# Column-block sums of three down-projection weights: from GpSimd additions in on-chip memory to adding transfers in device memory, one stage earlier

## The chip, the cores and the metric

One core of one Trainium2 chip runs the whole program. The metric is the device time of one execution in microseconds (us), as the median of repeated runs. In the texts PE is TensorE, DVE is VectorE, ACT is ScalarE, POOL is GpSimd and SP is SyncE, which in this kernel only issues transfers. "Device memory" is the chip's HBM, "on-chip memory" is SBUF.

## What is computed

The reference is a small language-model forward pass on one sequence of 512 tokens with a model width of 1024, all in float32. A first layer mixes tokens with three mixers (windowed attention, a state-space mixer, a gated delta-rule mixer), then comes a gated feed-forward block; two more layers with other mixers follow, each with a feed-forward block that has a short convolution. What matters here are the three feed-forward blocks. Cut to their core:

```python
# first block
f = (jax.nn.silu(h @ ffn_w_gate[l]) * (h @ ffn_w_up[l])) @ ffn_w_down[l]
x = x + rmsnorm(f, post_ffn_norm[l])
# the two later blocks: a = gated result of an up projection with a short convolution,
# then a @ w_down of the same shape
```

`ffn_w_down` is 2816 x 1024. So there are three down projections a (512 x 2816) times w (2816 x 1024), numbered n = 0, 1, 2 below.

## The kernel before, in words

**Order of stages.** (1) The input projection `w_in` with the three mixers woven into it, about 0 to 255 us of the span; (2) output projection; (3) up(0), the gate and up projection of block 0, followed by down(0), together about 306 to 650 us; (4) the second layer's mixer; (5) up(1) and down(1); (6) the third layer's mixer; (7) up(2) and down(2), which end the program. The engines run five separate instruction streams, each strictly in its own written order, tied by semaphores. In the mixer stages the order in which dense work (letter F) and mixer work (other letters) follow each other is a fixed string, the same on every engine (`first_order`, L258, walked by `walk`, L242).

**Weights.** Each weight arrives in chunks of at most 128 x 2048 float32 (1 MB), by a transfer that SP issues (`load`, L3367) into one of two buffers `raw`. TensorE works on pairs of high and low halves: ACT writes the high half `wH` (L1609), then DVE (L2274) or POOL (L3091) writes the low half `wL` = raw - wH. The set `BY_POOL` (L124) says for which chunks it is POOL: 1, 3 to 18, 52 to 68 and 111 to 116. Every product is then three matmuls (L681 to L683: high by high, high by low, low by high). A dense chunk of the input projection or of an up projection is two column tiles of eight such triples (`feat_side` on the other engines, L1488, which first prepares chunk c and then chunk c + 1). Two buffers each of `raw`, `wH` and `wL` serve in turn, so chunk c + 1 can be cast once TensorE has left chunk c - 1, and the load of chunk c + 2 is issued when the low half of chunk c is written (L3376).

**Down projection.** It is done as a two-by-two block product with seven block products in place of eight (Strassen's scheme in the form of Winograd). The weight is taken as four blocks of 1408 x 512, called b11, b12, b21 and b22; each is eleven blocks of 128 rows, numbered q. The scheme needs four sums of weight blocks (T1 to T4) and four sums of blocks of the activations (S1 to S4). The activation sums are made by POOL in `branch_sums` (L3035) during the up projection and in `down` (L3062) during the down projection. The weight sums are made in the same up projection by three functions:

- `stage` (SP, L3301) loads block row q of the weight, 1 MB, into the on-chip buffer `extra0`; it waits until the sums of q - 1 have been stored.
- `weight_sums` (POOL, L3050 to L3060) does four additions or subtractions of 128 x 512 in place.
- `store` (SP, L3310) writes `extra0` to `w_sums` (L284) in device memory.

Eleven such rounds fill up(n), whose 22 chunks carry them between their loads. The down projection reads `w_sums` back: `load_a` (L3330) for each q loads b11 from the weight and three sums from `w_sums`; `load_b` (L3343) later loads the fourth sum, then b12 and b21. Their buffers are the ring `raw_ring` (L446): raw[1], raw[0], extra1, extra0.

On TensorE `down` (L772) has first four products for each q, then three others. `partial`, `second`, `third`, `fifth` (DVE, L2183 to L2197), `add_f` (DVE, L2675) and `add_x` (POOL, L3069) add the products up after TensorE has written them.

**The first stage on POOL.** `dense` (L3096) runs `feat_side` for chunks 2 to 10, so POOL writes wL of chunk 3 first, then 4, 5 and so on, one for each chunk of TensorE. Between them `short` and `delta` put some mixer work on POOL (L3102, L3145).

Of the kernel before, what the change touches and what calls it, by code (L numbers as in the profile page):

```python
# [277 lines left out]
def build(nc, ins, out):  # L278
# [11 lines left out]
    with ctx:  # L290
# [276 lines left out]
        def sem(name):  # L567
# [7 lines left out]
        low_dve, low_pool = Line(sem("low_half_done_dve")), Line(sem("low_half_done_pool"))  # L575
        turned_pe, turned_hi, turned_lo = Line(sem("turned")), Line(sem("turned_high")), Line(sem("turned_low"))
        D = {n: Line(sem("dma_" + n), 16) for n in (
            "x0", "x1", "x2", "x3", "cols", "pm", "ident", "U", "brow", "lev", "abias", "ssd_nw", "gain", "oneh", "rb", "u_out", "u_rows", "staged", "stored",
            "row", "x_again", "CM", "wuk", "wuv", "far", "near", "cum_out", "cum0", "cum1", "cum2", "cum3", "sgg", "sgw", "sgb", "out")}
        pre, ev, gate, att, ssd, gdn0, gdn1, sums, mix, res, ffn, even, idx, unit, lat, odd, sgu, ln, dn = stages = [  # L580
            Marks(sem, n) for n in ("pre", "evac", "gate", "att", "ssd", "gdn0", "gdn1", "sums", "mix", "res", "ffn", "even", "index",
# [1568 lines left out]
        def dve_program(e):  # L2150
# [25 lines left out]
            def down(n, turn_tile, add_last, centre, finish):  # L2176

                for q in range(1, 11):
                    if q > 2:
                        low_outer(n, q - 3)  # L2180
                    low_a(n, q)

                def partial(name, j, bank, o, a):  # L2183
                    w.wait_ge(*dn.pe.at(n, bank[0], j))
                    e.tensor_tensor(o, a, q4v(ps[bank[1] + j][:, :]), ALU.add).then_inc(*dn.dve.one(n, name, j))

                def second(j):
                    w.wait_ge(*dn.act.at(n, "P1", j))
                    partial("P6", j, ("P6", 6), part(j, 1), part(j, 0))

                def third(j):
                    w.wait_ge(*dn.dve.at(n, "P6", j))
                    partial("P7", j, ("P7", 0), part(2 + j, 0), part(j, 1))

                def fifth(j):
                    w.wait_ge(*dn.dve.at(n, "P7", j))
                    partial("C22", j, ("P5", 2), part(2 + j, 1), part(2 + j, 0))  # L2197

                low_outer(n, 8)
                low_b(n, 0)  # L2200
                low_b(n, 1)
                second(0)
                second(1)
                low_outer(n, 9)
                third(0)
                third(1)
                low_b(n, 2)
                fifth(0)
                low_b(n, 3)
                fifth(1)  # L2210
                low_outer(n, 10)
                for v in range(4, 8):
                    low_b(n, v)
                add_last(2, 0, "P4", 6)
                low_b(n, 8)
                centre(2)
                finish(2)
                low_b(n, 9)
                add_last(3, 0, "P4", 6)
                low_b(n, 10)  # L2220
                centre(3)
                finish(3)
                for v in range(11, 14):
                    low_b(n, v)
                turn_tile(2)
                low_b(n, 14)
                low_b(n, 15)
                turn_tile(3)
                low_b(n, 16)
                add_last(0, 0, "P2", 4)  # L2230
                add_last(0, 1, "P3", 2)
                if n == 0:
                    split_done.add(51)
                    finish(0)
                    low_half(51, 0)
                    low_half(51, 1)
                    add_last(1, 0, "P2", 4)
                    add_last(1, 1, "P3", 2)
                elif n == 1:
                    split_done.update((101, 102))  # L2240
                    low_half(101, 0)
                    centre(0)
                    low_half(101, 1)
                    finish(0)
                    add_last(1, 0, "P2", 4)
                    low_half(102, 0)
                    add_last(1, 1, "P3", 2)
                    low_half(102, 1)
                    centre(1)
                else:  # L2250
                    centre(0)
                    finish(0)
                    add_last(1, 0, "P2", 4)
                    add_last(1, 1, "P3", 2)
                    centre(1)
                finish(1)
# [418 lines left out]
            def add_f(i, h, name, bank):  # L2675
                w.wait_ge(*dn.pe.at(0, name, i % 2))
                if i > 1 or h:
                    w.wait_ge(*dn.dve.at(0, "C22", i % 2))
                    e.tensor_tensor(part(i, h), part(i, h), q4v(ps[bank + i % 2][:, :]), ALU.add).then_inc(*dn.dve.one(0, name, i % 2))
                if i > 1:  # L2680
                    scale_f(i, 1)
                scale_f(i, h)
                if i > 1 or h:
                    w.wait_ge(*res.act.at("f", "sq", i, 0 if i > 1 else 1))
                    e.tensor_tensor(st[:, 24 + i:25 + i], st[:, 16 + 2 * i:17 + 2 * i], st[:, 17 + 2 * i:18 + 2 * i], ALU.add).then_inc(*res.dve.one("f", "sum", i))
# [345 lines left out]
        def pool_program(e):  # L3031
            w = Waits(e)
            split_done = set()

            def branch_sums(n, c0):  # L3035

                for m in range(22):
                    k = m % 11
                    if m % 2 == 0 and m < 20 or m == 19:
                        weight_sums(n, (m + 1) // 2)  # L3040
                    w.wait_ge(*ffn.dve.at("a", c0 + m))
                    if m < 11:
                        e.tensor_tensor(aR[:, k, 512:768], aR[:, k, 256:512], aR[:, k, 512:768], ALU.subtract).then_inc(*dn.pool.one(n, "S3", k))  # L3043
                    else:
                        w.wait_ge(*dn.pool.at(n, "S3", k))
                        e.tensor_tensor(aR[:, k, 768:1024], aR[:, k, 1280:1536], aR[:, k, 512:768], ALU.subtract).then_inc(*dn.pool.one(n, "S2", k))  # L3046
                        w.wait_ge(*dn.pool.at(n, "S2", k))
                        e.tensor_tensor(aR[:, k, 0:256], aR[:, k, 768:1024], aR[:, k, 256:512], ALU.add).then_inc(*dn.pool.one(n, "S1", k))

            def weight_sums(n, q):  # L3050

                b11, b12, b22, b21 = (extra0[:, 512 * j:512 * j + 512] for j in range(4))
                w.wait_ge(*D["staged"].at(n, q))
                e.tensor_tensor(b22, b22, b12, ALU.subtract).then_inc(*dn.pool.one(n, "T3", q))  # L3054
                w.wait_ge(*dn.pool.at(n, "T3", q))
                e.tensor_tensor(b12, b12, b11, ALU.subtract).then_inc(*dn.pool.one(n, "T1", q))
                w.wait_ge(*dn.pool.at(n, "T1", q))
                e.tensor_tensor(b11, b22, b11, ALU.add).then_inc(*dn.pool.one(n, "T2", q))
                w.wait_ge(*dn.pool.at(n, "T2", q))
                e.tensor_tensor(b21, b21, b11, ALU.subtract).then_inc(*dn.pool.one(n, "T4", q))  # L3060

            def down(n):  # L3062

# [5 lines left out]
                def add_x(i):  # L3069
                    if n:  # L3070
                        w.wait_ge(*ffn.act.at("x", n - 1, i))
                        w.wait_ge(*(dn.dve.at(n, "C22", i - 2) if i > 1 else dn.dve.at(n, "wlo", 12 + i)))
                        for h in (1, 0) if i > 1 else (1,):
                            xv = x[:, i, 512 * h:512 * h + 512]
                            e.tensor_tensor(q4v(xv), q4v(xv), part(i, h), ALU.add).then_inc(*dn.pool.one(n, "x", i, h))

                for i in HI_FIRST:
                    add_x(i)
# [16 lines left out]

            def dense():  # L3096
                for j in range(9):
                    yield from feat_side(C_IN + j, split, none)
                yield from tok_side([C_Z, C_Z + 1], True, split, none)
                yield "done"  # L3100
# [192 lines left out]
        def sp_program(e):  # L3293
# [4 lines left out]
                o = offs[DOWN[n]] + q * 128 * 2048  # L3298
                return ins["wbig"][o:o + 128 * 2048].rearrange("(p n) -> p n", p=128)[:, c0:c1]

            def stage(n, q):  # L3301

                if q:
                    w.wait_ge(*D["stored"].at(n, q - 1))
                else:
                    for p in [*(conv_start(n - 1) if n else ffn_start()), chunk_done(DOWN[n] - 23)]:
                        w.wait_ge(*p)
                e.dma_start(extra0[:, :], blocks(n, q, 0, 2048)).then_inc(*D["staged"].one(n, q))

            def store(n, q):  # L3310
                w.wait_ge(*dn.pool.at(n, "T4", q))
                e.dma_start(w_sums[n, q], extra0[:, :]).then_inc(*D["stored"].one(n, q))

            def up(n, c0, extra=None):

                split(c0)
                stage(n, 0)
                lead_side(c0, split, none, none)
                if extra:
                    extra(1)  # L3320
                for m in range(2, 22):
                    if m % 2 == 0 and m < 20 or m == 19:
                        store(n, (m + 1) // 2 - 1)
                        stage(n, (m + 1) // 2)
                    run(feat_side(c0 + m, split, none))
                    if extra:
                        extra(m)
                store(n, 10)

            def load_a(n, q):  # L3330

# [3 lines left out]
                    w.wait_ge(*ffn.dve.at("a", DOWN[n] - 1))  # L3335
                elif q > 3:
                    w.wait_ge(*dn.dve.at(n, "w23", q - 4))
                w.wait_ge(*D["stored"].at(n, 10 if q == 3 else q))
                line = raw_landed[A_RAW[q]]
                e.dma_start(raw_a(q)[:, 0:512], blocks(n, q, 0, 512)).then_inc(*line.one("first", n, q))  # L3340
                e.dma_start(raw_a(q)[:, 512:2048], w_sums[n, q, :, 0:1536]).then_inc(*line.one("a", n, q))
# [1 line left out]
            def load_b(n, r):  # L3343
# [1 line left out]
                w.wait_ge(*(dn.dve.at(n, "w23", 7 + r) if r < 4 else dn.dve.at(n, "wlo", (1, 3, 5, 7, 9)[r - 4])))  # L3345
                line = raw_landed[B_RAW[r]]
                if r < 3:
                    w.wait_ge(*D["stored"].at(n, 10))
                    ks, o, src = range(4 * r, min(4 * r + 4, 11)), 512, w_sums[n, :, :, 1536:2048].rearrange("k p n -> p k n")
                else:  # L3350
                    ks, o = range(2 * r - 6, min(2 * r - 4, 11)), 1024
# [308 lines left out]
```

## Time and profile before

| | |
|---|---|
| median of 3 runs | 1785.3 us (1784.28 to 1785.46) |
| the profiled execution's own time | 1785.67 us |
| span of the profiled execution, first to last instruction | 1783.8 us |
| outside the span | 1.9 us |
| busy, share of the span | PE 98%, DVE 65%, ACT 44%, POOL 37% |
| transfers | 270.83 MB, 152 GB/s over the span |
| mean granted clock of TensorE | 0.997 of full |

The span is what the rows below cover; all stages are placed by microseconds from its start. The 1.9 us outside are before the first and after the last instruction.

### The profile page before, as it was taken

The page shows a single profiled execution, that of the slowest core. Times are in us where ns is not written, and L with a number is a line of the kernel's source. Part 1 is how long each engine was busy: PE and PEld are TensorE (multiplying, and loading weights), DVE is VectorE, ACT ScalarE, POOL GpSimd, SP SyncE. Part 2 cuts the span into 40 slices and gives each one's busy share as a digit, 9 for nine tenths or more (in the row PEclk, how much of TensorE's full clock was granted, in tenths as well). Part 3 has the DMA queues.
Part 4 walks back from the last instruction along what each step waited for, and adds up shares of the span by engine and source line. Part 5 has one row for each costly group of instructions (what it writes and reads, how often), then busy time and mean ns, then how long its engine had stood idle before and what let it go on. Part 6 is the DMA issues. An engine that isn't in the chain of part 4 may idle for free.

```text
span 1783.8 us, 23185 instructions
## 1 busy us (share of the span) xinstructions
PE 1754.1 (98%) x9476; PEld 1448.8 (81%) x9476; DVE 1157.7 (65%) x1564; ACT 784.0 (44%) x1203; POOL 660.9 (37%) x434
## 2 busy tenths in 40 slices
PE   8999989999999999999999999999999999999998
PEld 7788978888888888666788888888788898888886
DVE  4687655323347857867657666689674467667798
ACT  6665345222225644556434433465333234333562
POOL 1443533332553114431243445532101344455431
PEclk9999999999999999999999999999999999999999
DMA  5212032654656533330225555574332245555663
GB/s 190 82 60 73 8 120 87 220 199 160 244 212 216 191 113 136 109 122 24 72 95 189 192 195 192 200 263 172 118 115 104 85 166 189 195 198 196 260 202 109
DMA packets 56548, 270.83 MB, mean 152 GB/s; under 512 B 5577, under 2 KB 11761, under 8 KB 34170
## 3 DMA queue, kind: packets, MB, share of 16 engines
q1 hardware_dynamic: 52090, 264.11, 41.8%
q10 hardware_dynamic: 4352, 5.24, 0.8%
q8 instruction: 75, 1.23, 0.3%
q14 instruction: 31, 0.25, 0.0%
HBM read 232.60 MB, written 38.30 MB: 152 GB/s over the span
## 4 chain that ended last, share of the span: by engine, by line
PE 91%; DVE 5%; ACT 2%; DMA 1%; issue 1%; POOL 1%; SPq 0%; ACTq 0%; DVEq 0%
PE ps L681 26%; PE ps L683 26%; PE ps L682 26%; PE ps L678 1%; PE ps L677 1%; PE ps L676 1%; PE ps L1312 1%; PE ps L1278 1%; PE ps L765 1%; PE ps L1271 1%; PE ps L1265 1%; DMA extra<-w_sums 1%; POOL wL L3091 1%; ACT wH L1609 1%; PE ps L1237 1%
## 5 line engine op out<-in xcount | busy, mean ns | idle before, releaser
L681 PE MATMUL ps<-hH,wH 128*128 128x512 f32 (+1 forms) x1560 | 593.5, 380 | 2.2 <-DVE gT L2321 0.9
L683 PE MATMUL ps<-hH,wL 128*128 128x512 f32 (+1 forms) x1560 | 587.0, 376 | 0.0
L682 PE MATMUL ps<-hL,wH 128*128 128x512 f32 (+1 forms) x1560 | 586.8, 376 | 0.0
L3091 POOL TENSOR_TENSOR wL<-raw,wH 128x1024 fp32r<-128x1024 f32 (+2 forms) x80 | 188.8, 2382 | 424.9 <-ACT wH L1609 417.4
L681 PEld LDWEIGHTS ps<-hH,wH 128*128 128x128 f32 x1560 | 293.9, 188 | 59.2 <-issue 3.4
L683 PEld LDWEIGHTS ps<-hH,wL 128*128 128x128 f32 x1560 | 293.6, 188 | 54.1
L682 PEld LDWEIGHTS ps<-hL,wH 128*128 128x128 f32 x1560 | 293.8, 188 | 51.6 <-issue 0.2
L1609 ACT ACTIVATE wH<-raw 128x1024 fp32r<-128x1024 f32 (+2 forms) x226 | 223.0, 1036 | 151.6 <-PE ps L683 143.9
L2274 DVE TENSOR_TENSOR wL<-raw,wH 128x1024 fp32r<-128x1024 f32 (+1 forms) x146 | 232.8, 1633 | 41.4 <-ACT wH L1609 41.4
L2884 DVE SCALAR_TENSOR_TENSOR ft<-ps,cols,ft 128x511 f32<-128x511 f32 (+1 forms) x176 | 131.6, 748 | 149.0 <-ACT ft L2063 145.8
L2063 ACT ACTIVATE ft<-ps,cols 128x512 f32<-128x512 f32 x88 | 60.6, 689 | 189.3 <-PE ps L683 189.3
L681 PE MATMUL ps<-wH,hH 128*128 128x512 f32 (+2 forms) x320 | 113.2, 354 | 3.3 <-DVE x L2917 1.6
L3054 POOL TENSOR_TENSOR extra<-extra 128x512 f32<-128x512 f32 x33 | 43.4, 1315 | 186.2 <-DMA extra<-in_wbig 186.2
L683 PE MATMUL ps<-wH,hL 128*128 128x512 f32 (+2 forms) x320 | 110.5, 345 | 0.0
L682 PE MATMUL ps<-wL,hH 128*128 128x512 f32 (+2 forms) x320 | 110.4, 345 | 0.0
L681 PE MATMUL ps<-wH,agH 128*128 128x512 f32 x264 | 102.9, 390 | 0.5 <-DVE wL L2160 0.5
L682 PE MATMUL ps<-wL,agH 128*128 128x512 f32 x264 | 102.7, 389 | 0.0
L683 PE MATMUL ps<-wH,agL 128*128 128x512 f32 x264 | 102.7, 389 | 0.0
L2663 DVE TENSOR_TENSOR aR<-ft,ps 128x512 f32<-128x512 f32 x22 | 15.1, 688 | 133.9 <-PE ps L683 133.9
L3067 POOL TENSOR_TENSOR aR<-aR 128x256 f32<-128x256 f32 x33 | 50.1, 1524 | 94.1 <-DVE agL L2165 94.1
L3043 POOL TENSOR_TENSOR aR<-aR 128x256 f32<-128x256 f32 x33 | 44.3, 1343 | 99.4 <-DVE aR L2893 68.8
L3046 POOL TENSOR_TENSOR aR<-aR 128x256 f32<-128x256 f32 x33 | 45.2, 1368 | 92.5 <-DVE aR L2893 59.1
(430 smaller groups left out, 2850.3 us busy)
## 6 DMA issues: line engine op xcount, KB each, us to landing
raw<-in_wbig SPq DMA_DIRECT2D x114, 1024.0 KB, 5.6
extra<-in_wbig SPq DMA_DIRECT2D x42, 1024.0 KB, 4.8
w_sums<-extra SPq DMA_DIRECT2D x33, 1024.0 KB, 8.7
raw<-w_sums SPq DMA_DIRECT2D x21, 768.0 KB, 6.5
extra<-w_sums SPq DMA_DIRECT2D x15, 768.0 KB, 7.1
rows<-in_rows SPq DMA_DIRECT2D x11, 512.0 KB, 8.0
raw<-in_wbig SPq DMA_DIRECT2D x18, 256.0 KB, 5.6
x<-in_x SPq DMA_DIRECT2D x8, 512.0 KB, 5.0
```

The source lines that it names most:

```text
L681: e.matmul(o, hi, m_hi, start=first, stop=False)
L682: e.matmul(o, hi, m_lo, start=False, stop=False)
L683: return e.matmul(o, lo, m_hi, start=False, stop=end)
L1609: e.activation(wH[r][:, cs], raw[r][:, cs], ACT.Copy).then_inc(*cast.one(c, h))
L2063: e.activation(ft[s][:, :], ps[b0 + t][:, :], ACT.Identity, scale=cols[:, column + 2:column + 3]).then_inc(*ffn.act.one("y", c, t))
L2274: e.tensor_tensor(wL[r][:, cs], raw[r][:, cs], wH[r][:, cs].bitcast(F32), ALU.subtract).then_inc(*low_dve.one(c, h))
L2884: e.scalar_tensor_tensor(y[:, d:512], ps[b0 + t][:, 0:512 - d], cols[:, column + 2 - d:column + 3 - d], y[:, d:512], ALU.mult, ALU.add).th ...
L3043: e.tensor_tensor(aR[:, k, 512:768], aR[:, k, 256:512], aR[:, k, 512:768], ALU.subtract).then_inc(*dn.pool.one(n, "S3", k))
L3046: e.tensor_tensor(aR[:, k, 768:1024], aR[:, k, 1280:1536], aR[:, k, 512:768], ALU.subtract).then_inc(*dn.pool.one(n, "S2", k))
L3054: e.tensor_tensor(b22, b22, b12, ALU.subtract).then_inc(*dn.pool.one(n, "T3", q))
L3067: e.tensor_tensor(aR[:, k, 768:1024], aR[:, k, 1024:1280], aR[:, k, 768:1024], ALU.subtract).then_inc(*dn.pool.one(n, "S4", k))
L3091: e.tensor_tensor(wL[r][:, cs], raw[r][:, cs], wH[r][:, cs].bitcast(F32), ALU.subtract).then_inc(*low_pool.one(c, h))
```

## The change

The sums are now made in device memory, by transfers that POOL issues. A plain transfer copies within device memory; a transfer with `accum_op=ALU.add` adds its source to what stands at its destination. Since these only add, the scheme is written so that all weight sums have plus signs: T1 = b11 + b12, T3 = b22 + b12, T2 = T3 + b11, T4 = T2 + b21 (before: differences). The signs go over to the activation sums and to the additions behind the products; the number, shape and engine of those instructions stay.

For each n there are twelve transfers, k = 0 to 11: six steps, each in two halves (block rows 0 to 5 and 6 to 10; 768 and 640 rows of device memory). Steps 0, 2 and 4 copy, steps 1, 3 and 5 add; steps 0 and 1 move two pieces of 512 numbers for each row, the others one. Each half has its own semaphore, and POOL waits for a half's previous step before it issues the next. For n = 0 they stand in `dense` of the first stage, two ahead of each of the chunks j = 1 to 6. For n = 1 and 2 they stand in `branch_sums` of up(0) and up(1), one ahead of each of the first twelve activation sums. `stage`, `store` and `weight_sums` are gone from SP and POOL.

```diff
-            "x0", ..., "u_rows", "staged", "stored",
+            "x0", ..., "u_rows", "block_sums0", "block_sums1",
...
-                def partial(name, j, bank, o, a):
+                def partial(name, j, bank, o, a, op=ALU.add):
...
-                    partial("P6", j, ("P6", 6), part(j, 1), part(j, 0))
+                    partial("P6", j, ("P6", 6), part(j, 1), part(j, 0), ALU.subtract)
...
-                    partial("C22", j, ("P5", 2), part(2 + j, 1), part(2 + j, 0))
+                    w.wait_ge(*dn.pe.at(n, "P5", j))
+                    e.tensor_tensor(part(2 + j, 1), q4v(ps[2 + j][:, :]), part(2 + j, 0), ALU.subtract).then_inc(*dn.dve.one(n, "C22", j))
...
-                    e.tensor_tensor(part(i, h), part(i, h), q4v(ps[bank + i % 2][:, :]), ALU.add).then_inc(*dn.dve.one(0, name, i % 2))
+                    if name == "P3":
+                        e.tensor_tensor(part(i, h), q4v(ps[bank + i % 2][:, :]), part(i, h), ALU.subtract).then_inc(*dn.dve.one(0, name, i % 2))
+                    else:
+                        e.tensor_tensor(part(i, h), part(i, h), q4v(ps[bank + i % 2][:, :]), ALU.add).then_inc(*dn.dve.one(0, name, i % 2))
...
+            def block_sums(n, k):
+
+                step, half = k // 2, k % 2
+                qs = slice(6 * half, 6 + 5 * half)
+                line = D[f"block_sums{half}"]
+                w_rows = ins["wbig"][offs[DOWN[n]]:offs[DOWN[n] + 1]].rearrange("(q p n) -> q p n", q=11, p=128)[qs].rearrange("q p n -> (q p) n")
+                s_rows = w_sums[n, qs].rearrange("q p n -> (q p) n")
+                t2, t1, t3, t4 = (slice(512 * a, 512 * a + 512) for a in range(4))
+                b11, b12, b22, b21 = t2, t1, t3, t4
+                if step:
+                    w.wait_ge(*line.at(n, step - 1))
+                if step == 0:
+                    o, a = s_rows[:, 512:1536].rearrange("r (h n) -> r h n", h=2), w_rows[:, 0:2048].rearrange("r (h n) -> r h n", h=2)[:, :, 0:512]
+                elif step == 1:
+                    o, a = s_rows[:, 512:1536].rearrange("r (h n) -> r h n", h=2), w_rows[:, b12].unsqueeze(1).broadcast_to([s_rows.shape[0], 2, 512])
+                else:
+                    o, a = ((s_rows[:, t2], s_rows[:, t3]), (s_rows[:, t2], w_rows[:, b11]),
+                            (s_rows[:, t4], s_rows[:, t2]), (s_rows[:, t4], w_rows[:, b21]))[step - 2]
+                if step in (1, 3, 5):
+                    e.dma_start(o, a, accum_op=ALU.add).then_inc(*line.one(n, step))
+                else:
+                    e.dma_start(o, a).then_inc(*line.one(n, step))
...
                 for m in range(22):
                     k = m % 11
-                    if m % 2 == 0 and m < 20 or m == 19:
-                        weight_sums(n, (m + 1) // 2)
+                    if n < 2 and m < 12:
+                        block_sums(n + 1, m)
...
-                        e.tensor_tensor(aR[:, k, 768:1024], aR[:, k, 1280:1536], aR[:, k, 512:768], ALU.subtract).then_inc(*dn.pool.one(n, "S2", k))
+                        e.tensor_tensor(aR[:, k, 768:1024], aR[:, k, 1280:1536], aR[:, k, 512:768], ALU.add).then_inc(*dn.pool.one(n, "S2", k))
                         w.wait_ge(*dn.pool.at(n, "S2", k))
-                        e.tensor_tensor(aR[:, k, 0:256], aR[:, k, 768:1024], aR[:, k, 256:512], ALU.add).then_inc(*dn.pool.one(n, "S1", k))
-
-            def weight_sums(n, q):
...
+                        e.tensor_tensor(aR[:, k, 0:256], aR[:, k, 256:512], aR[:, k, 768:1024], ALU.subtract).then_inc(*dn.pool.one(n, "S1", k))
...
-                            e.tensor_tensor(q4v(xv), q4v(xv), part(i, h), ALU.add).then_inc(*dn.pool.one(n, "x", i, h))
+                            e.tensor_tensor(q4v(xv), q4v(xv), part(i, h), ALU.add if i > 1 else ALU.subtract).then_inc(*dn.pool.one(n, "x", i, h))
...
             def dense():
                 for j in range(9):
+                    if 1 <= j < 7:
+                        block_sums(0, 2 * j - 2)
+                        block_sums(0, 2 * j - 1)
                     yield from feat_side(C_IN + j, split, none)
...
-            def stage(n, q):
...
-            def store(n, q):
...
-                stage(n, 0)
...
-                    if m % 2 == 0 and m < 20 or m == 19:
-                        store(n, (m + 1) // 2 - 1)
-                        stage(n, (m + 1) // 2)
...
-                store(n, 10)
...
                 elif q > 3:
                     w.wait_ge(*dn.dve.at(n, "w23", q - 4))
-                w.wait_ge(*D["stored"].at(n, 10 if q == 3 else q))
+                elif q == 3:
+                    for p in conv_start(n - 1) if n else ffn_start():
+                        w.wait_ge(*p)
+                w.wait_ge(*D[f"block_sums{q // 6}"].at(n, 3))
...
-                    w.wait_ge(*D["stored"].at(n, 10))
+                    for half in range(2):
+                        w.wait_ge(*D[f"block_sums{half}"].at(n, 5))
```

## Rows read from the trace of the kernel before

**Rows 1.** Busy time, share of the span and instructions of each engine.
```profile
PE 1754.1 (98%) x9476; PEld 1448.8 (81%) x9476; DVE 1157.7 (65%) x1564; ACT 784.0 (44%) x1203; POOL 660.9 (37%) x434
```
**Rows 2.** Windows: stretch; its length, busy per engine (instructions); clock; DMA share, GB/s.
```profile
240.00:250.00 10.00, 6.05 (x42) 5.21 (x42) 8.61 (x20) 3.72 (x10) 0.00 (x0) 0.82 0.03 11
250.00:255.00 5.00, 4.47 (x18) 3.52 (x17) 2.78 (x5) 3.59 (x5) 1.28 (x1) 0.68 0.34 115
...
306.00:546.00 240.00, 238.79 (x1128) 200.78 (x1127) 85.13 (x71) 62.02 (x73) 100.05 (x79) 1.00 0.54 196
545.00:650.00 105.00, 105.00 (x473) 86.99 (x471) 87.13 (x87) 65.08 (x83) 19.21 (x13) 1.00 0.54 193
...
920.00:1160.00 240.00, 239.59 (x1136) 201.66 (x1135) 159.76 (x157) 92.76 (x119) 117.29 (x77) 1.00 0.54 191
```
**Rows 3.** Waits of PE over the span, by releaser: total us, times, longest.
```profile
PE ps L862 <- DMA rows<-in_rows: 5.1, 1, 5.1
...
PE ps L681 <- POOL wL L3091: 0.8, 2, 0.4
```
**Rows 4.** Groups of POOL instructions by line: xcount, busy us, mean ns, idle before.
```profile
L3060 POOL TENSOR_TENSOR extra<-extra 128x512 f32<-128x512 f32 x33 | 56.5, 1713 | 2.6
...
L3054 POOL TENSOR_TENSOR extra<-extra 128x512 f32<-128x512 f32 x33 | 43.4, 1315 | 186.2 <-DMA extra<-in_wbig 186.2
```
**Rows 5.** POOL's timeline in the first stage: start us, length us, instructions.
```profile
36.84 4.76 POOL L3091 TENSOR_TENSOR wL<-raw,wH 128x1024 fp32r<-128x1024 f32 x2 [16.13 <-ACT wH L1609]
49.17 4.77 POOL L3091 TENSOR_TENSOR wL<-raw,wH 128x1024 fp32r<-128x1024 f32 x2 [7.57 <-ACT wH L1609]
63.05 5.22 POOL L3091 TENSOR_TENSOR wL<-raw,wH 128x1024 fp32r<-128x1024 f32 x2 [9.11 <-ACT wH L1609]
...
73.29 4.74 POOL L3091 TENSOR_TENSOR wL<-raw,wH 128x1024 fp32r<-128x1024 f32 x2
88.52 4.75 POOL L3091 TENSOR_TENSOR wL<-raw,wH 128x1024 fp32r<-128x1024 f32 x2 [10.49 <-ACT wH L1609]
105.20 5.19 POOL L3091 TENSOR_TENSOR wL<-raw,wH 128x1024 fp32r<-128x1024 f32 x2 [11.93 <-ACT wH L1609]
...
122.49 4.77 POOL L3091 TENSOR_TENSOR wL<-raw,wH 128x1024 fp32r<-128x1024 f32 x2
```
**Rows 6.** PE's timeline, the first matmul of each of chunks 4 to 9.
```profile
59.62 0.48 PE L681 MATMUL ps<-hH,wH 128*128 128x512 f32 x1
...
70.60 0.39 PE L681 MATMUL ps<-hH,wH 128*128 128x512 f32 x1
...
86.62 0.47 PE L681 MATMUL ps<-hH,wH 128*128 128x512 f32 x1
...
103.10 0.48 PE L681 MATMUL ps<-hH,wH 128*128 128x512 f32 x1
...
116.68 0.39 PE L681 MATMUL ps<-hH,wH 128*128 128x512 f32 x1
...
133.40 0.39 PE L681 MATMUL ps<-hH,wH 128*128 128x512 f32 x1
```
**Rows 7.** Transfers over the span: xcount, KB each, median us from issue to landing.
```profile
raw<-in_wbig SPq DMA_DIRECT2D x114, 1024.0 KB, 5.6
...
w_sums<-extra SPq DMA_DIRECT2D x33, 1024.0 KB, 8.7
```
**Rows 8.** Transfers, 428.9 to 440 us: busy tenths, GB/s in 40 slices; one issue.
```profile
DMA  0099409999997711111159799999921111111111
GB/s 0 0 236 177 118 0 413 472 443 443 384 413 325 295 59 44 55 44 55 50 227 428 310 458 463 458 458 458 428 79 44 44 44 44 44 44 50 44 44 44
...
u_rows<-u_scratch SPq DMA_DIRECT2D x1, 384.0 KB
```
**Rows 9.** Up(0): an issue of SP, a cast of ACT.
```profile
428.63 0.33 SPq L3377 DMA_DIRECT2D raw<-in_wbig  x1
...
435.01 2.01 ACT L1609 ACTIVATE wH<-raw 128x1024 fp32r<-128x1024 f32 x2 [4.90 <-PE ps L683]
```

More of the change, by code:

```diff
@@ L577, in build @@
         D = {n: Line(sem("dma_" + n), 16) for n in (
-            "x0", "x1", "x2", "x3", "cols", "pm", "ident", "U", "brow", "lev", "abias", "ssd_nw", "gain", "oneh", "rb", "u_out", "u_rows", "staged", "stored",
+            "x0", "x1", "x2", "x3", "cols", "pm", "ident", "U", "brow", "lev", "abias", "ssd_nw", "gain", "oneh", "rb", "u_out", "u_rows", "block_sums0", "block_sums1",
             "row", "x_again", "CM", "wuk", "wuv", "far", "near", "cum_out", "cum0", "cum1", "cum2", "cum3", "sgg", "sgw", "sgb", "out")}
@@ L2181, in down @@
                     low_a(n, q)
-                def partial(name, j, bank, o, a):
+                def partial(name, j, bank, o, a, op=ALU.add):
                     w.wait_ge(*dn.pe.at(n, bank[0], j))
-                    e.tensor_tensor(o, a, q4v(ps[bank[1] + j][:, :]), ALU.add).then_inc(*dn.dve.one(n, name, j))
+                    e.tensor_tensor(o, a, q4v(ps[bank[1] + j][:, :]), op).then_inc(*dn.dve.one(n, name, j))
                 def second(j):
                     w.wait_ge(*dn.act.at(n, "P1", j))
-                    partial("P6", j, ("P6", 6), part(j, 1), part(j, 0))
+                    partial("P6", j, ("P6", 6), part(j, 1), part(j, 0), ALU.subtract)
                 def third(j):
@@ L3045, in branch_sums @@
                         w.wait_ge(*dn.pool.at(n, "S3", k))
-                        e.tensor_tensor(aR[:, k, 768:1024], aR[:, k, 1280:1536], aR[:, k, 512:768], ALU.subtract).then_inc(*dn.pool.one(n, "S2", k))
+                        e.tensor_tensor(aR[:, k, 768:1024], aR[:, k, 1280:1536], aR[:, k, 512:768], ALU.add).then_inc(*dn.pool.one(n, "S2", k))
                         w.wait_ge(*dn.pool.at(n, "S2", k))
-                        e.tensor_tensor(aR[:, k, 0:256], aR[:, k, 768:1024], aR[:, k, 256:512], ALU.add).then_inc(*dn.pool.one(n, "S1", k))
-            def weight_sums(n, q):
[L3052 to L3060, printed above, removed]
+                        e.tensor_tensor(aR[:, k, 0:256], aR[:, k, 256:512], aR[:, k, 768:1024], ALU.subtract).then_inc(*dn.pool.one(n, "S1", k))
             def down(n):
@@ L3299, in blocks @@
                 return ins["wbig"][o:o + 128 * 2048].rearrange("(p n) -> p n", p=128)[:, c0:c1]
-            def stage(n, q):
[L3303 to L3308, printed above, removed]
-            def store(n, q):
-                w.wait_ge(*dn.pool.at(n, "T4", q))
-                e.dma_start(w_sums[n, q], extra0[:, :]).then_inc(*D["stored"].one(n, q))
             def up(n, c0, extra=None):
                 split(c0)
-                stage(n, 0)
                 lead_side(c0, split, none, none)
```

## The prediction

> **What bounds the kernel now.** I read the busy shares first: PE is busy 1754.1 of 1783.8 us [rows 1], so every change that only frees another engine has 29.7 us to win over the whole program. The windows say where that is not: in up(0) and down(0) PE idles 1.2 us of 345, in up(1) 0.4 of 240 [rows 2]. These are the stages from which POOL's additions and SP's staging transfers go. The waits of PE name POOL with 0.8 us in all; the longest single one, 5.1 us, is for a first load at the start, which the change does not touch [rows 3]. So the bound is TensorE's own stream, and the question is whether the new work, which is waited for on POOL, reaches it.
>
> **What goes.** 4 x 33 POOL instructions of 1.3 to 1.7 us [rows 4], about 196 us of POOL time, all in up stages. They released only the stores. 33 loads and 33 stores on SP go with them. Value on the path: at most the 1.6 us of idle in these windows [rows 2]; I take 0. The first load of the down projection's ring that could have waited for the last store waits anyway for the last activation tile or stands behind one that does. The changed signs keep number, engine and shape of every addition: 0. The added wait for P5 in `fifth` was inside `partial` before: 0.
>
> **What comes, by size.** A float is 4 bytes. Steps 0 and 1 write 768 x 2 x 512 numbers = 3.15 MB in the first half and 2.62 MB in the second; steps 2 to 5 write 1.57 and 1.31 MB. For one n that is 23 MB written, half of it by copies, half by adding.
>
> *Rate of a copy.* The only copy within device memory, u_rows, kept two of the sixteen engines busy (a tenth) at 44 to 47 GB/s, so 22 to 23.5 each; sixteen would give up to 376 GB/s, if nothing behind them is shared. That is the upper end. The same rows show at most 463 GB/s in one direction when all sixteen work [rows 8]. A copy reads and writes, an addition reads twice and writes. If those streams share some 460 GB/s, and the weight loads keep taking 1.05 MB for each chunk of some 14 us (75 GB/s), then about 380 is left: 190 GB/s of copied and 127 GB/s of added bytes. The lower end is a store's median, 1.05 MB in 8.7 us or 120 GB/s, landing time and queueing included [rows 7]; for adding, half of that, 60. I take 190 and 127, as they come from a rate seen with all sixteen engines; both ends stay for the range. A landing adds 2 to 3 us to the moving (a 1.05 MB load lands in 5.6 us [rows 7], at 420 to 460 GB/s it moves in 2.4); I take 2.
>
> The Trainium skill (DMA: Bandwidth & Descriptors, the table of latency and other measured facts) gives 214 GB/s per direction as the full rate of copies between tensors in device memory. By it my sum below would be about 13 us smaller than with 190; no row here shows such a copy on sixteen engines.
>
> *Price of an issue on POOL.* No row has one. SP's take 0.33 us [rows 9]; that is the low end. POOL must also make a read and a write entry for each of up to 1536 pieces of 2 KB. Its fastest of the four old sums pays 1315 ns for 512 columns [rows 4], 2.6 ns each; I take 1 us + 2.5 ns a piece: 4.8 and 4.2 us for steps 0 and 1, 2.9 and 2.6 us for the rest. High end: 7.5 ns a piece.
>
> **First stage, n = 0: the place that decides.** Behind each waiting transfer POOL's queue holds wL of the next chunk, for which PE waits. POOL writes wL(4) at 49.2, wL(5) at 63.1, wL(6) at 73.3, wL(7) at 88.5, wL(8) at 105.2, wL(9) at 122.5 [rows 5]; PE starts those chunks at 59.6, 70.6, 86.6, 103.1, 116.7, 133.4 [rows 6]. It needs only the first of the two instructions, 2.6 us. Slack: 59.6 - 51.8 = 7.8 us, then 4.9, 10.7, 12.0, 8.9, 8.3. The mixer's other instructions on POOL (5 us before wL(6), some 8 before wL(9)) shift along.
>
> Transfers run one after the other on the engines; a pair of one step can be passed only when both halves of the step before have landed.
> - Step 0: issued 41.6 (end of wL(3)) to 50.6; moved by 59.2 and 73.0; landed 61 and 75. wL(4) at 50.6: no stall.
> - Step 1: issued 61 and 75; POOL is free at 79.2. wL(5)'s first half is there at 81.8, needed at 70.6: **stall 11.2**. Moving takes 24.8 + 20.7 us: landed 99.7 and 120.4.
> - Step 2: second half issued at 120.4; wL(6) at 125.6, needed at 86.6 + 11.2 = 97.8: **stall 27.8** (39.0 so far). Moved by 133.5, landed 135.5.
> - Step 3: issued by 138.1; wL(7) at 140.7, needed at 142.1: none. Landed 147.9 and 158.2.
> - Step 4: issued by 160.8; wL(8) at 163.4, needed at 155.7: **stall 7.8**. Landed 173.4.
> - Step 5: issued by 179.2, behind the mixer's instructions; wL(9) at 181.8, needed at 180.1: **stall 1.6**.
>
> Sum 48.4 us. A long idle also costs clock: at 240 to 255 us, after PE had fallen under two thirds busy, the granted clock was 0.82 for 10 us and 0.68 for 5 [rows 2], a loss of 0.18 x 10 + 0.32 x 5 = 3.4 us between the two levels (1.2 and 2.4 GHz). Three stalls: up to 10. Against it, other chains catch up meanwhile and part of the 4.5 us that PE idles at 240 to 255 [rows 2] may shrink; I take 4 off. **Sum: 48.4 + 10 - 4 = 54 us slower.** Against the profiled execution's own 1785.67 (span 1783.8 and 1.9 around it) that is 1840; the median, 1785.3, is 0.4 lower, so 1840 stands.
>
> **Up stages, n = 1 and 2.** The same waits stand on POOL, before activation sums that nobody needs until the down projection. Ten transfers must land before POOL is through: 11.5 MB copied at 190 and 8.7 added at 127 are 61 + 68 us, with landings about 150, well inside the 240 us of the stage. Cost 0. Weight loads share the engines: one issued at 428.6 is cast on ACT at 445.9, two casts after 424.1 with 10.9 us between them [rows 9], so 17.3 us for a landing of 5.6; cover of nearly 12. If that cover went, each load too late by 1 us would cost PE that microsecond, over about twelve chunks twice.
>
> **Rivals.**
> (a) *Hidden anyway; not slower.* Place: POOL between wL(3) and wL(5). If copies keep u_rows' rate on sixteen engines (376 GB/s) and adding runs at 250 or more, step 0 lands by 53 and 59 us, step 1 by 75, and the stalls are 0 to 2 us: 1785 to 1787. It decides at the pass of step 1: stalls start when its second issue ends later than about 68 us. For it: the first stage moves only some 75 GB/s. Against it: the share argument. Between this and the forecast, 376 with 188 gives 9 us and 300 with 200 gives 11: 1790 to 1800.
> (b) *Adding far slower.* 120 with 80 or 60 GB/s gives stalls of 121 or 157 us, with clock 1915 to 1955; the up stages then last 205 to 240 us on POOL, just inside. With 190 and half of it, 95, the stalls sum to 71 us: 1865. The Trainium skill (Collectives: The Full Stack, on why a reducing step runs at half the gathering one) lays such a half rate to two reads on one ring; by it the last figure holds.
> (c) *POOL's own issue time.* With 7.5 ns a piece and fast transfers (376 both) stalls are 44 us, at 10 ns 72: the same end by another road, 1835 to 1870. It would show as long busy issues in place of waits.
> (d) *PE fills the gaps with mixer work.* The written order excludes it: behind the first matmul of a chunk everything on PE waits too. No chance given.
>
> **How the numbers follow.** A measurement of this kernel tells about 0.2% (3.6 us) from no change. Faster by more needs idle time that the removed work caused; the windows leave 2 us: 0.03. Rival (a) proper: 0.17. Slower by more: 0.80, made of 0.17 between (a) and the forecast, 0.40 for the forecast and (c) (1810 to 1875), 0.23 above that, a third of which I leave out past 1935. Range 1785 to 1935; the likeliest case alone 1810 to 1875.
>
> **What would show it.** Right: POOL waits for transfers before L3091 between 55 and 180 us, PE's waits name POOL wL L3091 with tens of us, chunk 6 starts near 125, and both up stages keep 240 us. Wrong: step 1 landed by 80 us; or long POOL issues; or PE idle in up(0), which would mean that weight loads starve. The pattern of the copies' GB/s in the first stage settles the rates.

## The result, and the profile after

The changed kernel takes 1838.95 us (median of 4 runs, 1835.57 to 1841.73) against 1785.38 us: a ratio of 1.0298, 95% interval 1.0286 to 1.0310. The forecast was 1840. The profiled execution has a span of 1833.7 us, 49.9 more than before. It is the shortest of the four, so the rows below explain 49.9 of the 53.6 us between the medians.

The total is as forecast, but it is not made up as forecast. Half of it arose where I had put nothing. The views show that in this order.

The busy shares of the kernel after (they answer to [rows 1]):
```profile
PE 1762.0 (96%) x9476; PEld 1453.0 (79%) x9476; DVE 1120.9 (61%) x1564; ACT 783.4 (43%) x1203; POOL 514.9 (28%) x338
```
POOL's busy time fell by 146 us: some 196 us of additions went, and the issues of the 36 transfers, which are counted here, brought about 50. PE's idle time grew from 29.7 to 1833.7 - 1762.0 = 71.7 us, by 42.0; its busy time grew by 7.9 us with the same number of instructions, as its granted clock was lower (0.984 over the span against 0.997 before, 0.77 from 60 to 110 us, where the longest wait lies). 42.0 + 7.9 = 49.9.

Windows of the kernel after: the first stage and the output projection up to up(0), up(0) itself, and the rest (columns as in [rows 2]):
```profile
0.00:320.00 320.00, 284.05 (x2211) 241.85 (x2212) 184.25 (x330) 154.62 (x285) 127.51 (x87) 0.95 0.54 153
...
355.00:595.00 240.00, 219.48 (x951) 180.81 (x950) 68.92 (x60) 52.52 (x61) 40.96 (x41) 0.96 0.64 170
595.00:1834.00 1239.00, 1225.14 (x6071) 999.05 (x6069) 849.38 (x1153) 558.67 (x831) 328.20 (x203) 1.00 0.43 140
```
In up(0) PE idles 20.5 us; [rows 2] had 1.2. From 595 us on it idles 13.9 us, as before (1238.0 - 1224.59 = 13.4 for the same stretch). A landmark gives the shares of the 49.9 us. POOL writes wL of the same chunk, at the end of the output projection, at 295.65 before and here:
```profile
320.40 5.37 POOL L3106 TENSOR_TENSOR wL<-raw,wH 128x1024 fp32r<-128x1024 f32 x2 [14.21 <-ACT wH L1609]
```
So 24.8 us are lost by then, 21.1 of them idle time of PE and 3.6 longer matmuls. The first cast of down(0) on ACT stands at 583.4 here and 533.8 before, so up(0) adds another 24.8 us (20.5 and 4.3); the first cast of down(1) is 49.5 late, and nothing is added there. Up(1), with the same twelve transfers, costs nothing.

Waits of PE over the span after (as [rows 3]):
```profile
PE ps L681 <- DVE wL L2275: 22.2, 3, 12.5
PE ps L681 <- POOL wL L3106: 19.1, 4, 16.5
PE ps L862 <- DMA rows<-in_rows: 5.1, 1, 5.1
```
Two causes of nearly the same size: low halves from POOL (forecast) and low halves from DVE (not forecast).

**First stage.** POOL's timeline after (as [rows 5]; the lines with DMA_DIRECT2D are the issues, L3060 a copy, L3058 an addition; the time in brackets is how long POOL sat idle before, and for what):
```profile
39.88 3.33 POOL L3060 DMA_DIRECT2D w_sums<-in_wbig  x2
49.04 4.76 POOL L3106 TENSOR_TENSOR wL<-raw,wH 128x1024 fp32r<-128x1024 f32 x2 [5.83 <-ACT wH L1609]
56.68 3.17 POOL L3058 DMA_DIRECT2D w_sums<-in_wbig  x1 [2.88 <-DMA w_sums<-in_wbig]
67.23 2.71 POOL L3058 DMA_DIRECT2D w_sums<-in_wbig  x1 [7.38 <-DMA w_sums<-in_wbig]
68.74 5.90 POOL L3106 TENSOR_TENSOR wL<-raw,wH 128x1024 fp32r<-128x1024 f32 x2
...
88.29 0.76 POOL L3060 DMA_DIRECT2D w_sums<-w_sums  x1 [8.61 <-DMA w_sums<-in_wbig]
104.38 0.68 POOL L3060 DMA_DIRECT2D w_sums<-w_sums  x1 [15.33 <-DMA w_sums<-in_wbig]
105.07 4.66 POOL L3106 TENSOR_TENSOR wL<-raw,wH 128x1024 fp32r<-128x1024 f32 x2
```
The reader is to see the second issue of each pair waiting for a transfer, and wL, in the queue behind it, following at once: wL(5) at 68.7 (before 63.1), wL(6) at 105.1 (before 73.3). PE's timeline has the price:
```profile
107.56 0.77 PE L681 MATMUL ps<-hH,wH 128*128 128x512 f32 x1 [16.46 <-POOL wL L3106]
```

**Up(0).** ACT's casts wait for weight loads:
```profile
432.56 2.00 ACT L1609 ACTIVATE wH<-raw 128x1024 fp32r<-128x1024 f32 x2 [21.21 <-DMA raw<-in_wbig]
...
479.73 2.00 ACT L1609 ACTIVATE wH<-raw 128x1024 fp32r<-128x1024 f32 x2 [25.76 <-DMA raw<-in_wbig]
```
The two loads were issued at 398.0 and 440.6. The first one's line in its source view (the landing is from issue to data):
```profile
L3381 SPq DMA_DIRECT2D raw<-in_wbig x1: 9534/9534/9534, 398.0 to 398.0; - x1
...
DMA to landing us min/median/max: 34.6/34.6/34.6
```
The issue of this load alone kept SP busy for 9.5 us (9534 ns); most others take 0.33. The second load took 39.1 us. The two loads that follow these two took 27.7 and 31.7. All others of up(0) from 354 us until the sums are done land in 8.5 to 11.1 us, and those of up(1), beside the same steps, in 8.2 to 10.8. The price on PE, which needs the low half that DVE makes from such a load:
```profile
435.02 0.76 PE L681 MATMUL ps<-hH,wH 128*128 128x512 f32 x1 [7.98 <-DVE wL L2275]
...
482.19 0.77 PE L681 MATMUL ps<-hH,wH 128*128 128x512 f32 x1 [12.54 <-DVE wL L2275]
```
What SP had issued just ahead of the slow two, 10.5 and 4.2 us earlier, is in its timeline:
```profile
387.47 0.73 SPq L3458 DMA_DIRECT2D u_rows<-u_scratch  x1
...
436.41 0.62 SPq L3458 DMA_DIRECT2D u_rows<-u_scratch  x1
```
These are the first two of four copies on two of the sixteen transfer engines [rows 8]; the other two come when the sums are nearly or quite done, and up(1) has none. That gave theory A: the first stage is late by POOL's queue, up(0) by u_rows meeting POOL's transfers.

### The profile page after: what moved, and what is told of

Read it like the earlier page. It is cut to its first block, busy times and chain, and to the rows that moved or that the text cites. A ratio compares the mean times of both kernels' runs of the same rounds, so it can differ in the third digit from the quotient of the medians.

```text
span 1833.7 us, 23033 instructions
## 1 busy us (share of the span) xinstructions
PE 1762.0 (96%) x9476; PEld 1453.0 (79%) x9476; DVE 1120.9 (61%) x1564; ACT 783.4 (43%) x1203; POOL 514.9 (28%) x338
## 4 chain that ended last, share of the span: by engine, by line
PE 83%; DMA 8%; DVE 5%; ACT 2%; POOL 1%; issue 1%; SPq 0%; ACTq 0%; DVEq 0%
PE ps L681 24%; PE ps L683 23%; PE ps L682 23%; DMA raw<-in_wbig 4%; DMA w_sums<-in_wbig 3%; PE ps L678 1%; PE ps L676 1%; PE ps L677 1%; PE ps L1312 1%; PE ps L1278 1%; POOL wL L3106 1%; ACT wH L1609 1%; PE ps L765 1%; PE ps L1271 1%; PE ps L1265 1%
## 5 line engine op out<-in xcount | busy, mean ns | idle before, releaser
L681 PE MATMUL ps<-hH,wH 128*128 128x512 f32 (+1 forms) x1560 | 596.6, 382 | 42.5 <-DVE wL L2275 20.5
L2275 DVE TENSOR_TENSOR wL<-raw,wH 128x1024 fp32r<-128x1024 f32 (+1 forms) x146 | 198.6, 1400 | 79.6 <-ACT wH L1609 79.6
L3073 POOL TENSOR_TENSOR aR<-aR 128x256 f32<-128x256 f32 x33 | 44.4, 1345 | 277.9 <-DVE aR L2897 168.4
L3070 POOL TENSOR_TENSOR aR<-aR 128x256 f32<-128x256 f32 x33 | 39.2, 1189 | 164.5 <-DVE aR L2897 134.9
L3082 POOL TENSOR_TENSOR aR<-aR 128x256 f32<-128x256 f32 x33 | 51.0, 1552 | 93.5 <-DVE agL L2165 93.5
L681 PEld LDWEIGHTS ps<-wH,hH 128*128 128x128 f32 x320 | 60.8, 190 | 12.1 <-DVE wL L2275 1.9
```

Of the source, the lines that this page charges most:

```text
L681: e.matmul(o, hi, m_hi, start=first, stop=False)
L2275: e.tensor_tensor(wL[r][:, cs], raw[r][:, cs], wH[r][:, cs].bitcast(F32), ALU.subtract).then_inc(*low_dve.one(c, h))
L3082: e.tensor_tensor(aR[:, k, 768:1024], aR[:, k, 1024:1280], aR[:, k, 768:1024], ALU.subtract).then_inc(*dn.pool.one(n, "S4", k))
```

## The experiments

All times are medians; ratios are to the kernel before on the same chip. Eight kernels ran.

### Apart: u_rows on sixteen engines, sums in their own stage

The first edit turns the order of the dimensions of the four u_rows copies:

```diff
-   e.dma_start(bass.AP(u_rows.tensor, h * 128 * 385, [[128 * 385, 2], [385, 128], [1, 384]]),
-               bass.AP(u_dram.tensor, h * 384, [[384, 2], [0, 128], [1, 384]]))
+   e.dma_start(bass.AP(u_rows.tensor, h * 128 * 385, [[385, 128], [128 * 385, 2], [1, 384]]),
+               bass.AP(u_dram.tensor, h * 384, [[0, 128], [384, 2], [1, 384]]))
```


> The changed kernel, but the four u_rows copies of up(0) have their dimension of 128 rows outermost, so that all sixteen transfer engines share them; same bytes. Theory A: the second half of the loss (24.8 us by landmarks, in up(0)) comes from weight loads queued behind u_rows on the two engines that u_rows uses, where it must share with POOL's adding transfers. Then up(0) keeps 240 us, weight loads there land within 12 us, and the median is 1838.95 - 24.8 = about 1814 us; the first stage stays 24.8 us late. Rival B: POOL's transfers starve the weight loads by bandwidth, with or without u_rows: landings of 30 us stay and the time stays at 1830 or more.

Measured: 1812.96 us, ratio 1.0157 (1.0143 to 1.0171), 26.0 us less than the changed kernel. The first stage of its profiled execution is 27.0 us late by the landmark above. Weight loads in up(0) land in 8.4 to 11.7 us while the sums run, and in up(0) PE waits for DVE's wL no more. The forecast of theory A held; so the traffic of the sums by itself is covered, and rival B falls.

The second edit makes each n's twelve transfers in its own stage, up(n), and so takes those of n = 0 out of the first stage:
```diff
-                    if n < 2 and m < 12:
-                        block_sums(n + 1, m)
+                    if m < 12:
+                        block_sums(n, m)
...
-                    if 1 <= j < 7:
-                        block_sums(0, 2 * j - 2)
-                        block_sums(0, 2 * j - 1)
```


> The changed kernel with each n's twelve transfers in its own up stage (n in up(n)), none in the first stage. Theory A: the first stage returns to its times of before (wL of chunk 6 at 73 us), up(0) keeps its loss of some 25 us as u_rows still uses two engines: 1810 to 1816 us; the sums land some 150 us into the stage, 90 before they are read. Rival B': the first stage's delay is from something else that came with the change (PE chunk 6 still starts 20 us or more late, 1835). Rival C: sums made in their own stage come too late for the down projection, and its first product waits by 5 us or more.

Measured: 1796.16 us, 1.0065 (1.0050 to 1.0079). The first stage is back where it was (the landmark stands at 295.69). My figure was missed: 10.9 us are lost between the medians, not 25. The profiled execution, the shortest of the four, is 7.8 us longer than before, and PE waits for wL from DVE for 5.8 of them in up(0). The load behind the first u_rows (at 362.7 us) landed in 19.1 us, the one behind the second (397.8) in 32.4, the one behind the third (442.2) in 18.7. So 24.8 is not a constant of the stage. What sets the size stays open. The steps that stand beside u_rows do not tell it alone: the first u_rows comes 2.8 us before POOL passes step 1's first half and 22.8 before it passes the second, in the changed kernel 2.5 and 20.4, and yet the load behind it took 19.1 us here and 34.6 there. The sums come in time: no wait of PE for one releaser from down(0) on sums to more than 1.8 us, and rival C falls too.

Both edits together:

> Both edits of the two runs before: sums in their own up stage, u_rows on sixteen engines. Theory A: the two losses are the whole loss and add: 1785 to 1787 us, within 0.2% of the kernel before, with POOL busy some 145 us less than in the kernel before. If a third loss exists it is what remains above 1787. A gain of more than 2 us would mean that the staging of before had cost something that its waits did not show; I expect none.

Measured: 1785.21 us, 1.0002 (0.9993 to 1.0011), from 11 runs. PE waits for the same things in this run as in the kernel before; POOL is named with 0.8 us, as before. The three largest:
```profile
PE ps L862 <- DMA rows<-in_rows: 5.0, 1, 5.0
PE ps L1007 <- DVE yall L2450: 3.3, 2, 2.8
PE ps L1271 <- DVE least L2799: 1.8, 4, 1.0
```
and its busy shares are
```profile
PE 1754.1 (98%) x9476; PEld 1448.6 (81%) x9476; DVE 1110.7 (62%) x1564; ACT 783.6 (44%) x1203; POOL 511.5 (29%) x338
```
PE's 1754.1 is the number of before to the digit. So the two losses are the whole loss, and making the sums by transfers frees 149 us of POOL with no measurable change of the time.

> The kernel before with u_rows alone put on sixteen engines. Theory A: there u_rows costs nothing, as no adding transfers share its two engines and the cover of 12 us suffices: within 1 us of the kernel before, 1785. If u_rows already cost something, it is faster by that.

Measured: 1785.37 us, 0.9999 (0.9990 to 1.0009). In the kernel before, u_rows on two engines cost nothing that can be measured.

### What the first stage pays for

Both runs here stand on the first one (u_rows on sixteen engines, 1812.96 us). In this one the adding steps copy, so the sums are not made, while source, destination and bytes written stay:
```diff
-                    e.dma_start(o, a, accum_op=ALU.add).then_inc(*line.one(n, step))
+                    e.dma_start(o, a).then_inc(*line.one(n, step))
```


> e1 (changed kernel with u_rows on sixteen engines, 1812.96 us) with the three adding steps made plain copies of the same source and destination; so the weight sums are left out and the kernel computes something else in the down projections. Theory: in the first stage POOL's wait is as long as the transfers take, and an addition takes longer than a copy as it reads twice: the traces so far give about 235 GB/s of copied and 155 of added bytes, and the forecast's chain worked with 235 for both gives 10 us of stalls in place of 24: about 1799 us, and landings of steps 1 and 3 shorter by a third. Rival: the waits are set by something other than the bytes read (issue, order): 1810 or more.

Measured: 1795.52 us, 1.0057 (1.0041 to 1.0074). The same landmark as above stands at 305.81, 10.2 us late in place of 27.0 in the run that it stands on; my chain with both rates at 235 had 10 of stalls. PE's longest wait for POOL's wL is 5.6 us in place of 19.1, and wL(6) comes at 91.4:
```profile
90.75 0.67 POOL L3060 DMA_DIRECT2D w_sums<-w_sums  x1 [9.31 <-DMA w_sums<-in_wbig]
91.44 4.66 POOL L3106 TENSOR_TENSOR wL<-raw,wH 128x1024 fp32r<-128x1024 f32 x2
```
Step 1, issued at 57.4 and 67.3, landed at 80.4 and 90.4; as an addition, in the changed kernel, it landed at 88.0 and 104.1. POOL's issue of step 1 fell as well, from 3.17 to 1.67 us; the edit changes both at once, but 1.5 us is small beside the 14 us of landing. So the length of the additions carries more than half of the first stage's delay.

Here the low halves of chunks 4 to 9 go to DVE:
```diff
-BY_POOL = {1} | set(range(3, 19)) | ...
+BY_POOL = {1, 3} | set(range(10, 19)) | ...
```


> e1 with the low halves of chunks 4 to 9 written by DVE in place of POOL; the transfers and their waits stay where they are. Theory: the first stage is late because wL stands behind the waits in POOL's queue. Then with wL elsewhere its delay goes, less what 12 more DVE instructions of 1.2 us cost there: 1786 to 1795 us. Rival: the transfers slow the weight loads or the engines themselves: 1805 or more.

Measured: 1799.76 us, 1.0083 (1.0068 to 1.0099): between the theory's range and the rival's. No wait for wL from POOL is left in the first stage, which is 17.3 us late here in place of 27.0 (12.2 of more idle time of PE, 5.1 of longer matmuls). In its place stands the next thing behind POOL's waits:
```profile
PE ps L1065 <- POOL XT L3185: 8.9, 1, 8.9
```
and POOL's timeline of this run shows why:
```profile
130.01 0.72 POOL L3060 DMA_DIRECT2D w_sums<-w_sums  x1 [9.54 <-DMA w_sums<-in_wbig]
139.32 0.68 POOL L3060 DMA_DIRECT2D w_sums<-w_sums  x1 [8.59 <-DMA w_sums<-in_wbig]
139.98 0.54 POOL L3180 MEMSET P<- 128x512 f32 x1
...
141.19 1.27 POOL L3185 TENSOR_TENSOR XT<-lev,XT 128x512 f32<-128x512 f32 x1
```
The mixer's XT, at 111.8 us in the kernel before, comes at 141.2. So POOL's queue still holds PE up, by something else than wL, and no wait of PE names a weight load. The rest of the idle time is in waits for DVE, the largest 1.9 and 2.4 us (0.9 of the latter before); why they grew was not looked into. I had expected the wL to be all that PE waits for there.

### What up(0) pays for

> The changed kernel with u_rows still on two engines, but issued after chunks 16 to 19 of up(0), when POOL's twelve transfers have landed. Theory A: the cost in up(0) is the meeting of the two; apart they cost nothing: 1813 us as e1. Rival: two busy engines alone delay weight loads past their cover: 1825 or more.

The edit is `if m in (16, 17, 18, 19)` in place of `(5, 8, 11, 14)`, with h as 2 * (m - 16). Measured: 1812.47 us, 1.0154 (1.0139 to 1.0169). Loads land in 11.2 us or less. Without the sums beside it a copy on two engines costs nothing that can be measured; the loss needs both.

In the last one the same four copies, with the pattern of before (two parts) and three of them while the sums run, are issued by ACT in its loop over m in place of SP:
```diff
             for m in range(2, 22):
                 run(feat_side(C_UP + m, split, ffn_tile(C_UP + m, 2 * (m % 2))))
+                if m in (5, 8, 11, 14):
+                    h = 2 * (m - 5) // 3
+                    e.dma_start(bass.AP(u_rows.tensor, h * 128 * 385, [[128 * 385, 2], [385, 128], [1, 384]]),
+                                bass.AP(u_dram.tensor, h * 384, [[384, 2], [0, 128], [1, 384]])).then_inc(*D["u_rows"].one())
```


> The changed kernel with u_rows on two engines at nearly the same times, but issued by ACT, so that it stands in another queue than SP's weight loads. Theory A1: the weight load waits because it stands behind u_rows in SP's own queue on those two engines; then its landing falls under 17 us and the time to about 1813. Theory A2: it is the share of the two engines, whatever the queue: landings of 30 us stay and so does 1835 or more. Between them: part of each.

Measured: 1812.33 us, 1.0152 (1.0136 to 1.0167). ACT's timeline has the copy where SP had it,
```profile
391.48 1.18 ACTq L1892 DMA_DIRECT2D u_rows<-u_scratch  x1
```
and the load that SP issued 9 us later shows
```profile
L3385 SPq DMA_DIRECT2D raw<-in_wbig x1: 328/328/328, 400.5 to 400.5; - x1
...
DMA to landing us min/median/max: 10.6/10.6/10.6
```
34.6 us behind u_rows in SP's queue, 10.6 beside it in another queue, with the same pattern and bytes. No load of up(0) in this run takes more than 11.1 us. That settles A1 against A2: the weight load stood behind u_rows in SP's own queue. That POOL's transfers were what made u_rows slow there is inferred: without them (the run before this one) the loads land in time. The time of u_rows itself was not seen. The Trainium skill (DMA: Bandwidth & Descriptors, Queues, rings and completion order) says that each transfer engine consumes a queue's entries in order and takes turns between queues; these two landings agree.

## Why the prediction came out right, and which of its steps were wrong

The bound and what goes away: right. PE's stream sets the time; 149 us less on POOL gained nothing in the version without the two losses, which takes as long as the kernel before.

The mechanism of the first stage: right. Waits in POOL's queue hold up wL, the worst at wL(6). Its size was not. I summed stalls of 11.2, 27.8, 7.8 and 1.6 us, 48.4 in all, with 6 us net for clock and catching up. Measured is 24.8 us with the clock in it: waits for wL of 1.8 and 16.5 us, 2.8 of other idle time, and 3.6 of longer matmuls where I had put 10. The terms that were mis-sized are the two rates, 190 and 127 GB/s. Step 0, 5.77 MB issued from 39.9 us, had landed by 66.9; step 1, another 5.77 MB, filled the 37.2 us to 104.1. That is about 240 GB/s for copies (24 us of moving, with my 2 us of landing taken off) and 155 for additions. With 235 and 155, and issues at their measured length, the forecast's own chain gives three stalls of about 3, 20 and 1, some 24 us. The waits for wL were 18.3, so the chain still gives too much; and as the rates were read from this run, that is a check of the chain and not of the rates. A fifth to a quarter on the rates halves its result, since each wait only counts beyond a slack of 5 to 12 us.

The argument of shared streams had the ratio right: three streams against two make 0.67, and 155 to 240 is 0.65. Its size was too low. 240 GB/s copied are 480 of reading and writing, 155 added are 465, so by this estimate the streams shared some 470 GB/s beside the weight loads, not 380. The rate of 376 GB/s that u_rows' two engines would give on sixteen was not reached. The figure of 214 GB/s that the Trainium skill (DMA: Bandwidth & Descriptors, Latency and other measured facts) has for copies was below the measured rate too, but nearer. The 13 us that the forecast hung on it come only if the additions are raised in step with it, to 143 GB/s; with the copies alone its chain gives 5.

Issue price: 4.8 and 4.2 us taken for steps 0 and 1, 2.9 and 2.6 for the rest. The issues take 1.5 to 1.9 us for a copy of two pieces a row, 3.17 and 2.71 for an addition of two, 0.7 for a copy and 1.1 to 1.2 for an addition of one. Rival (c) needed several times that, so it falls.

"Up stages: cost 0": wrong, and the step that failed is the sentence on the weight loads. It took 5.6 us as the landing and asked how far the sums would stretch it for loads in general. For general loads the cover held, as up(1) shows. It did not ask what stands ahead of a load in SP's own queue. The trace of before had a sign of it: at 429.0 SP issued u_rows, and the store issued right behind it, at 429.6, took 15.0 us to land against a median of 8.7 [rows 7], while from some 437 us on only two engines were busy [rows 8]. I read those rows for a rate alone. Weight loads were not held up before: the ones behind the four u_rows were issued 10.7 to 16.0 us after them and landed in 6.5 to 7.1 us. At the 44 to 47 GB/s of [rows 8] a u_rows takes some 8 to 9 us (an estimate), so it was through by then. With the sums beside it the load behind it took 34.6 and 39.1 us, past the lead of 17.3.

Rival (a) decided as said: the second issue of step 1 ended at 69.9 us, just past the limit of 68, and the stall there was 1.8 us. But step 2's pass, at 105 us, was the larger one. Rival (b) falls with the additions' 155 GB/s, which is 0.65 of the copies' rate and not half. So the point forecast hit within 1.1 us by two errors of 25 to 30 us with opposite signs, 54 put in the first stage where 25 to 27 arose and 0 in up(0) where 25 to 26 did. That is luck, and the likeliest case's range held the time for a reason that was half the true one.

## What to carry to other kernels

A transfer issued from an engine's compute queue can cost that queue far more by the wait that orders it behind the one before than by its issue; list every instruction behind such a wait, and what TensorE needs of it, before placing it between two weight halves. A transfer that runs on two engines can hold back the sixteen-engine transfer behind it in the same queue, and did so here by 25 to 30 us once other traffic was beside it; give such copies an outer dimension that spreads them, or another queue. When bulk traffic is added, look for the slowest transfer ahead of a load, not for the mean bandwidth.

## What the runs showed of the hardware beyond expectation

- Copies within device memory on sixteen engines: 5.77 MB in about 24 us, 240 GB/s, with weight loads beside them (339 GB/s moved in all from 42 to 57 us). Additions: 155 GB/s of result in the first stage (219 in all from 67 to 88 us).
- POOL's issue of an addition takes 1.7 to 1.9 times that of a copy of the same pieces (3.17 and 2.71 us against 1.85 and 1.50; the same two steps made copies took 1.67 and 1.48).
- DVE's busy time fell by 37 us, which I had not looked for, and by 47 in the version with both edits. Its groups of low halves, of the kernel before and then after:
```profile
L2274 DVE TENSOR_TENSOR wL<-raw,wH 128x1024 fp32r<-128x1024 f32 (+1 forms) x146 | 232.8, 1633 | 41.4 <-ACT wH L1609 41.4
```
```profile
L2275 DVE TENSOR_TENSOR wL<-raw,wH 128x1024 fp32r<-128x1024 f32 (+1 forms) x146 | 198.6, 1400 | 79.6 <-ACT wH L1609 79.6
```
  The same 146 instructions took 1633 ns in the kernel with POOL's additions and 1400 in the one without, 34 of the 37 us. The low halves of the down projections (L2160, x36), beside which no such additions run, took 1535 in both. DVE is off the path here; where it is the bound, this would count. The staging loads and stores went away together with the additions, and no run was made to part the two, so the cause is not shown.
- The clock's share: 7.9 us of longer matmuls for 42 us more of idle time, in stretches of which the longest were 16.5, 12.5 and 8.0 us. The forecast had counted 10 for the first stage alone, which took 3.6.
- How long u_rows itself took on its two engines beside the sums was not measured. If the load behind it cannot land first, the landings (432.6 and 479.7) bound it by 45 and 43 us.
